# Attention of a hybrid diffusion step: heads in pairs on halves of the TensorE array, exponentials multiplied on VectorE

## What is computed

```python
def block_attention(q, k, v):
    ...
    scale = ATT_HD ** -0.5
    def one_block(qi):
        s = jnp.einsum('bqhgd,bkhd->bhgqk', qi, k, preferred_element_type=jnp.float32) * scale
        p = jax.nn.softmax(s, axis=-1).astype(v.dtype)
        return jnp.einsum('bhgqk,bkhd->bqhgd', p, v)
    ...
def odd_mixer(h, w_in, w_out, q_norm_w, k_norm_w, ctx_k=None, ctx_v=None):
    q, k, v = _split(h @ w_in, (ATT_Q, ATT_KV, ATT_KV))
    q = rmsnorm(q.reshape(b, t, ATT_HEADS, ATT_HD), q_norm_w)
    k = rmsnorm(k.reshape(b, t, ATT_KV_HEADS, ATT_HD), k_norm_w)
    ...
    if ctx_k is None:
        o = block_attention(q, k, v)
    else:
        q, k = axial_rope(q), axial_rope(k)
        o = block_attention(q, jnp.concatenate([ctx_k, k], axis=1), jnp.concatenate([ctx_v, v], axis=1))
    return o @ w_out, k, v
```

## Time and profile before

| | us |
|---|---|
| median of 3 runs | 3247.36 (3247.33 to 3247.4) |
| the profiled execution | 3248.14 |
| its span, first to last instruction | 3246.3 |
| TensorE busy | 3073.5 (95%) |
| VectorE busy | 1614.3 (50%) |
| ScalarE busy | 762.0 (23%) |
| GpSimd busy | 223.7 (7%) |

### The profile page before, as it was taken

How to read it: one execution, slowest core, us unless ns; L and a number is a source line. 1 busy time by engine, 2 the same in 40 slices (tenths; PEclk the granted TensorE clock), 3 DMA queues, 4 the chain that set the end, 5 groups by cost and what they waited for, 6 DMA issues and landing times.

```text
span 3246.3 us, 49355 instructions
## 1 busy us (share of the span) xinstructions
PE 3073.5 (95%) x20119; PEld 2896.3 (89%) x20119; DVE 1614.3 (50%) x2517; ACT 762.0 (23%) x939; POOL 223.7 (7%) x195
## 2 busy tenths in 40 slices
PE   7999998998989898999998999998989998999997
PEld 5999998998378888999998999998966668999997
DVE  6777565351355544777766752225343434222324
ACT  3212122222111122311222312113113442212122
POOL 2000000000033240000000000000003330000000
PEclk9999999996689989999999999999977998999999
DMA  7554332221000002355343332222100001222221
GB/s 242 156 156 142 120 118 76 75 67 47 10 1 1 0 8 78 116 156 151 124 139 107 116 96 73 78 72 71 65 31 1 1 1 52 65 78 78 66 71 52
DMA packets 306184, 256.04 MB, mean 79 GB/s; under 512 B 9100, under 2 KB 267272, under 8 KB 306056
## 3 DMA queue, kind: packets, MB, share of 16 engines
q1 hardware_dynamic: 306056, 254.26, 25.6%
HBM read 250.56 MB, written 3.67 MB: 78 GB/s over the span
## 4 chain that ended last, share of the span: by engine, by line
PE 90%; DVE 4%; issue 3%; ACT 2%; POOL 1%; DMA 0%; SPq 0%; DVEq 0%; POOLq 0%; ACTq 0%
PE ps L297 70%; PE ps L1593 2%; PE ps L1616 2%; PE ps L1286 2%; PE ps L709 2%; PE ps L1298 2%; PE ps L1296 1%; PE ps L1604 1%; PE ps L1063 1%; PE ps L736 1%; PE ps L1047 1%; PE ps L899 1%; POOL pr L1721 1%; PE ps L367 0%; PE ps L482 0%
## 5 line engine op out<-in xcount | busy, mean ns | idle before, releaser
L297 PE MATMUL ps<-h_hi,w_hi 128*128 128x320 f32 x3712 | 851.9, 311 | 22.7 <-DVE h_lo L533 16.4
L297 PE MATMUL ps<-h_lo,w_hi 128*128 128x320 f32 x3712 | 850.4, 310 | 0.0
L297 PE MATMUL ps<-h_hi,w_lo 128*128 128x320 f32 x3712 | 849.3, 310 | 0.0
L297 PEld LDWEIGHTS ps<-h_hi,w_hi 128*128 128x128 f32 x3712 | 624.4, 189 | 24.5 <-issue 24.4
L297 PEld LDWEIGHTS ps<-h_lo,w_hi 128*128 128x128 f32 x3712 | 625.3, 189 | 0.0
L297 PEld LDWEIGHTS ps<-h_hi,w_lo 128*128 128x128 f32 x3712 | 624.8, 189 | 0.0
L270 ACT CAST w_hi<-w_raw 128x2048 fp32r<-128x2048 f32 x164 | 311.6, 1900 | 542.9 <-PE ps L297 542.9
L277 DVE TENSOR_TENSOR w_lo<-w_raw,w_hi 128x2048 fp32r<-128x2048 f32 x164 | 375.5, 2290 | 92.1 <-ACT w_hi L270 91.8
L297 PE MATMUL ps<-hid_hi,w_hi 128*128 128x320 f32 x1408 | 321.8, 310 | 0.0
L297 PE MATMUL ps<-hid_lo,w_hi 128*128 128x320 f32 x1408 | 320.9, 309 | 0.0
L297 PE MATMUL ps<-hid_hi,w_lo 128*128 128x320 f32 x1408 | 320.6, 309 | 0.0
(11 more groups left out here) (241 smaller groups left out, 2663.0 us busy)
## 6 DMA issues: line engine op xcount, KB each, us to landing
w_raw<-in_ffn_w_in_dram SPq DMA_DIRECT2D x176, 512.0 KB, 5.0
mod_raw<-in_mod_w_dram SPq DMA_DIRECT2D x64, 1024.0 KB, 5.2
w_raw<-in_ffn_w_out_dram SPq DMA_DIRECT2D x64, 512.0 KB, 4.4
w_raw<-in_even_w_in_dram SPq DMA_DIRECT2D x28, 512.0 KB, 4.3
w_raw<-in_ffn_w_out_dram SPq DMA_DIRECT2D x32, 384.0 KB, 3.7
mod_first<-in_mod_w_dram SPq DMA_DIRECT2D x8, 1024.0 KB, 14.3
w_raw<-in_odd_w_in_dram SPq DMA_DIRECT2D x12, 512.0 KB, 4.3
w_raw<-in_even_w_out_dram SPq DMA_DIRECT2D x8, 512.0 KB, 4.1
```

Of the source, the lines that this page charges most:

```text
L297: mm = nc.tensor.matmul(ps[:, 4 * s + 2 * n + b, 0:HALF], w[s][:, k, cols], v[:, k, b * HALF:(b + 1) * HALF], start=(first and k == 0), st ...
```

## The change

Attention takes two heads at a time, the two of one query tile. For pair u (8 a block, 40 in all, written out without a loop):

- `scores` reads the queries straight from `proj` (no staging copy). The first head of the pair uses partitions 0 to 63 and banks 0 and 1, the second partitions 64 to 127 and banks 2 and 3; their matmuls alternate, in pieces of 256, 256 and 128 keys. They wait until both exponentials of pair u - 1 are done.
- The query norm's weight is multiplied by 1/8 once, ahead of the norms, so that the scores come scaled. VectorE's reduction writes the negated maximum itself; L1687 is gone.
- `exps` runs once for each head, into four buffers `pr`, which are now the scratch tiles `TMP`.
- `inverse` (VectorE) inverts a head's sum and multiplies the exponentials in place; `pool_attention` is gone.
- `turn` transposes both heads, ten tiles into banks 4, 5 and 7. ScalarE copies four tiles of the first head; VectorE the fifth of both, then four of the second.
- `values` alternates between the heads, which write partitions 0 to 63 and 64 to 127 of bank 6. The output is split every four pairs, 512 columns at a time.

```diff
-        q_st = over_u("q_st", [P, DT, P], 18432)
-        pt = [over_u(f"pt{s}", [P, 5 * P], 22528 + 2560 * s) for s in range(2)]
-        pr = [over_u(f"pr{s}", [P, 5 * P], 27648 + 2560 * s) for s in range(2)]
+        pt = [over_u(f"pt{s}", [P, 2, 5 * P], 22528 + 5120 * s) for s in range(2)]
+        pr = TMP
...
             dve.wait_ge(oc_in, 80)
+            nc.vector.tensor_scalar(qk_w[:, 0:1], qk_w[:, 0:1], ASCALE, None, ALU.mult).then_inc(qw_ready, 1)
             dve_tnorm_rec(dve, "odd_qk")
+            dve.wait_ge(qw_ready, 1)
...
+        PAIRS = AH // 2
+        UNITS = PAIRS * TT
...
+        def pair_pieces(kt):
+
+            if kt == 1:
+                return ((0, 0, P), (1, 0, P))
+            return ((0, 0, 256), (1, 0, 256), (0, 256, 512), (1, 256, 512), (0, 512, T), (1, 512, T))
...
+            def scores(u):
+                n, p, kt = pair_at(u)
+                if u == 0:
+                    pe.wait_ge(qr_step, 3 * DT)
+                else:
+                    pe.wait_ge(at_p, 2 * u)
+                for hh, c0, c1 in pair_pieces(kt):
+                    q = slice(64 * hh, 64 * hh + 64)
+                    k0 = P if n else 0
+                    mm = nc.tensor.matmul(psf[:, hh * 1024 + c0:hh * 1024 + c1], proj[q, p, n * P:(n + 1) * P],
+                                          keys[q, p // 2, k0 + c0:k0 + c1], start=True, stop=True)
                 mm.then_inc(at_s, 1)
...
+            def turn(u):
+                n, p, kt = pair_at(u)
+                pe.wait_ge(at_norm, 2 * u + 2)
+                if u:
+                    pe.wait_ge(at_ta, u)
+                    pe.wait_ge(at_td, u)
+                for hh in range(2):
+                    for i in range(kt):
+                        o = ((4 + hh) * 512 + i * P) if i < 4 else 7 * 512 + hh * P
+                        mm = nc.tensor.transpose(psf[:, o:o + P], pr[2 * (u % 2) + hh][:, i * P:(i + 1) * P], ident[:, :])
                 mm.then_inc(at_t, 1)
...
+                if p % 4 == 0 and u:
+                    pe.wait_ge(at_lo, u // 4)
+                o = 6 * 512 + (p % 4) * P
                 for i in range(kt):
+                    for hh in range(2):
+                        mm = nc.tensor.matmul(psf[64 * hh:64 * hh + HD, o:o + P],
+                                              vals[:, (1 + i if n else 0), (p // 2) * HD:(p // 2 + 1) * HD],
+                                              pt[u % 2][:, hh, i * P:(i + 1) * P], start=(i == 0), stop=(i == kt - 1))
                 mm.then_inc(at_o, 1)
...
+            scores(0)
+            for u in range(UNITS):
+                if u + 1 < UNITS:
+                    scores(u + 1)
+                turn(u)
+                if u:
+                    values(u - 1)
+            values(UNITS - 1)
...
+            def exps(u):
+                n, p, kt = pair_at(u)
+                for hh in range(2):
+                    h = 2 * p + hh
+                    act.wait_ge(at_neg, 2 * u + hh + 1)
+                    if u >= 2:
+                        act.wait_ge(at_t, u - 1)
+                    nc.scalar.activation(pr[2 * (u % 2) + hh][:, 0:kt * P], psf[:, hh * 1024:hh * 1024 + kt * P], ACT.Exp,
+                                         bias=a_neg[:, h:h + 1], accum_out=a_den[:, h:h + 1]).then_inc(at_p, 1)
...
+            def maxima(u):
+                n, p, kt = pair_at(u)
                 dve.wait_ge(at_s, u + 1)
+                for hh in range(2):
+                    h = 2 * p + hh
+                    nc.vector.tensor_reduce(a_neg[:, h:h + 1], psf[:, hh * 1024:hh * 1024 + kt * P], AX.X, ALU.max,
+                                            negate=True).then_inc(at_neg, 1)
+
+            def inverse(u, hh):
+                h = 2 * pair_at(u)[1] + hh
+                dve.wait_ge(at_p, 2 * u + hh + 1)
+                nc.vector.reciprocal(a_rec[:, h:h + 1], a_den[:, h:h + 1]).then_inc(at_rec, 1)
+                dve.wait_ge(at_rec, 2 * u + hh + 1)
+                v = pr[2 * (u % 2) + hh][:, 0:pair_at(u)[2] * P]
+                nc.vector.tensor_scalar(v, v, a_rec[:, h:h + 1], None, ALU.mult).then_inc(at_norm, 1)
...
+            for u in range(UNITS):
+                if u + 1 < UNITS:
+                    maxima(u + 1)
+                    inverse(u + 1, 0)
+                w = min(4, pair_at(u)[2]) * P
+                dve.wait_ge(at_t, u + 1)
+                if u >= 2:
+                    dve.wait_ge(at_o, u - 1)
+                if w > P:
+                    nc.vector.tensor_copy(pt[u % 2][:, :, 4 * P:5 * P], ps[:, 7, 0:2 * P].rearrange("p (h n) -> p h n", h=2))
+                nc.vector.tensor_copy(pt[u % 2][:, 1, 0:w], ps[:, 5, 0:w]).then_inc(at_td, 1)
+                if u + 1 < UNITS:
+                    inverse(u + 1, 1)
+                if u and u % 4 == 0:
+                    outputs(u // 4 - 1)
...
-            pool_attention(pool)
```

More of the change, by code:

```diff
@@ L1557, in dve_odd_prep @@
                 nc.vector.tensor_tensor(q, q, rt[j % 2][:, :], ALU.add).then_inc(qr_step, 1)
-        def blocks(eng, body):
-            body(0, None, 1, 5)
-            body(1, 1, 5, 5)
-            with eng.Fori(2, TT - 1) as n:
-                body(n, 5, 5, 5)
-            body(TT - 1, 5, 5, None)
-        def after(eng, s, v):
-            if not isinstance(v, int) or v > 0:
-                eng.wait_ge(s, v)
-        def unit(n, h, tk, tn):
-            return (n, h, tk) if h < AH else (n + 1, h - AH, tn)
@@ L1580, in pe_attention @@
-        def pe_attention(pe):
-            def scores(n, h, kt):
-                if kt is None:
-                    return
-                u = AH * n + h
-                if h == 0:
-                    pe.wait_ge(q_staged, n + 1)
-                after(pe, at_p, u - 1)
-                q = slice(64 * (h % 2), 64 * (h % 2) + 64)
-                o = 2 * (h % 2) * 512
-                k0, w = (0 if kt == 1 else P), kt * P
-                for c in range(0, w, 512):
-                    e = min(c + 512, w)
-                    mm = nc.tensor.matmul(psf[:, o + c:o + e], q_st[q, h // 2, :], keys[q, h // 4, k0 + c:k0 + e],
-                                          start=True, stop=True)
-                mm.then_inc(at_s, 1)
-            def turn(n, h, kt):
-                u = AH * n + h
-                pe.wait_ge(at_norm, u + 1)
-                after(pe, at_ta, u)
-                after(pe, at_td, u)
-                for i in range(kt):
-                    o = 4 * 512 + i * P
-                    mm = nc.tensor.transpose(psf[:, o:o + P], pr[h % 2][:, i * P:(i + 1) * P], ident[:, :])
+        PAIRS = AH // 2
@@ L1619, in values @@
                 mm.then_inc(at_o, 1)
-            def body(n, tp, tk, tn):
-                for h in range(AH):
-                    scores(*unit(n, h + 2, tk, tn))
-                    if h:
-                        values(n, h - 1, tk)
-                    elif tp:
-                        values(n - 1, AH - 1, tp)
-                    turn(n, h, tk)
             pe.wait_ge(ck_out, 1)
             pe.wait_ge(kr_step, 16)
-            for h in range(2):
-                scores(0, h, 1)
-            blocks(pe, body)
@@ L1716, in pool_attention @@
-        def pool_attention(pool):
-            def body(n, tp, tk, tn):
-                for h in range(AH):
-                    pool.wait_ge(at_rec, AH * n + h + 1)
-                    v = pr[h % 2][:, 0:tk * P]
-                    nc.gpsimd.tensor_tensor(v, v, a_rec[:, h:h + 1].to_broadcast([P, tk * P]), ALU.mult).then_inc(at_norm, 1)
-            blocks(pool, body)
+            scores(0)
[5 more added lines that the diff above has]
+                    values(u - 1)
@@ new lines, in pe_attention, with outputs @@
+            values(UNITS - 1)
+        def act_attention(act):
+            def exps(u):
[7 more added lines that the diff above has]
+                                         bias=a_neg[:, h:h + 1], accum_out=a_den[:, h:h + 1]).then_inc(at_p, 1)
+            def outputs(j):
+                n, t = j // 2, 4 * (j % 2)
+                act.wait_ge(at_o, 4 * j + 4)
+                nc.scalar.copy(h_hi[:, t:t + 4, n * P:(n + 1) * P],
+                               ps[:, 6, :].rearrange("p (t n) -> p t n", t=4)).then_inc(at_hi, 1)
+            exps(0)
+            for u in range(UNITS):
+                if u + 1 < UNITS:
+                    exps(u + 1)
+                w = min(4, pair_at(u)[2]) * P
+                act.wait_ge(at_t, u + 1)
+                if u >= 2:
+                    act.wait_ge(at_o, u - 1)
+                nc.scalar.copy(pt[u % 2][:, 0, 0:w], ps[:, 4, 0:w]).then_inc(at_ta, 1)
+                if u and u % 4 == 0:
+                    outputs(u // 4 - 1)
+            outputs(UNITS // 4 - 1)
@@ L1742, in pe_odd @@
             pe_attention(pe)
-            pe.wait_ge(at_lo, TT)
+            pe.wait_ge(at_lo, 2 * TT)
             pe_linear(pe, "odd_out", 4, None)
```

103 lines of the change are left out of this document (23 added, 80 removed).

## The result

The changed kernel takes **3143.03 us** (median of 4 runs, 3135.53 to 3144.01) against 3247.35 of the kernel before on the same chip: a ratio of **0.9676, 95% interval 0.966 to 0.9693**. The forecast was 3158 with a range from 3143 to 3195, so the direction was right, and the time lies at the very edge of the range's fast end: the gain is 104 us, and 89 were expected. The profiled run is the one of 3144.01 us.

A forecast was written before the change was run, and what follows sets the result against it. TensorE's phases were taken to bound the latent blocks, VectorE after the change. Context 22 + 32 pairs x 4.3 + clock 7 + end 3 = 169.6 us for a stage of 259.3, giving 3158 us; range 3143 to 3195.

The forecast's parts named there:

- The halves: Attention's matmuls on TensorE: both halves of the array overlap; a latent pair's scores 1.28 to 1.48 us, values 1.26.
- Score halves that take turns: Rival, 10%: row halves don't overlap in the scores; 5.2 us a latent pair, 3187 us in all (3180 to 3195).
- The rival of loads that show: Rival, 2%: each of a pair's 20 value records waits for its weight load; 5.7 us a pair, 3202 us.
- A latent round: One pair of heads in the latent blocks: 4.3 us expected against 6.42 for two heads before; ends 4.05 and 4.8.
- the loop through three engines: Latent pair: next scores wait for both exponentials; scores, first reduction, exponentials and way back take 4.03 us, 4.23 with overhang.
- two loops of nearly the same length that hand work to each other cost a little more than either: Latent pair: VectorE's 4.2 us and the way through the engines, 4.03 to 4.23, together taken as 4.3.
- The context block: First 8 pairs of attention, at the lower clock: 2.7 us a pair, 22 us in all against 28.
- The clock: Start of the latent blocks: clock still low for 2.5 pairs, 2.8 us extra each, 7 us; near full speed afterwards.
- The end: After the last latent pair: values, then the half-size split on ScalarE and VectorE one after another, 3 us.
- everything going well: Forecast's own fast end: 4.05 us a latent pair, 1.74 a context pair and an early clock rise, 3140 us.
- The slower case: Rival, 10%: clock stays low in the latent blocks; 7.7 us a pair, 3260 us (3232 to 3273).
- What would show it: Signs in latent rounds: multiplications 0.55 us, VectorE hardly idle, scores 1.3 to 1.5, values 1.2 to 1.3, rounds 4.2 to 4.4, GpSimd empty.

## Where the prediction was right and where not

*The halves.* Right: scores 1.35 (1.28 to 1.48 expected), values 1.31 (1.26), transposes 1.25 to the values (1.23). Score halves that take turns, the 10% rival, would need about 2.4; even head by head they took 1.89. The rival of loads that show is refuted in the round above: the pair's 20 loads of the whole height take 1.07 us beside 1.31 of matmuls. The Trainium skill ("TensorE: Matmul & The Clock Gate", Part 3, The mechanism) says that a weight load overlaps running matmuls only when its row group differs; these rows disagree with it too, since by it the values would have taken some 2.1 us more (an estimate, 20 loads of 0.106 us). The same section of the Trainium skill also has loads pulled ahead into a background weight buffer, which the rows would fit; no run here can show it.

*A latent round.* Right in kind: VectorE and the loop through three engines, 4.04 and 4.03 to 4.23 by the working, measured 4.03. "VectorE becomes the bound" came true by 0.06 us: the other loop is 3.97. A first step that failed is "two loops of nearly the same length that hand work to each other cost a little more than either": with the split they cost 4.18, which is VectorE's sum of 4.04 + 0.15, not 4.3. Term: 32 x 4.3 = 137.6, measured 133.8.

*The context block.* The step that failed here is the overlap: the term of 2.7 us a pair was too large. The timeline of one, at the lower clock:

```profile
2420.44 0.80 PE L1588 MATMUL ps<-keys,proj 64*128 64x128 f32 x4
...
2421.29 0.49 DVE L1665 TENSOR_REDUCE a_neg<-ps 128x1 f32<-128x128 f32 x2
2421.61 0.37 ACT L1637 ACTIVATE tmp_b<-ps,a_neg 128x128 f32<-128x128 f32 x1 [1.07 <-DVE a_neg L1665]
...
2422.47 0.80 PE L1588 MATMUL ps<-keys,proj 64*128 64x128 f32 x4
```

The round is 2.03: scores, first reduction (0.32 to the exponentials, not 0.5), exponentials. I had laid inverse, multiplication and copy end to end behind them; they lie beside the next round's scores. From the end of the rotation to the first latent scores at 2431.07 it is 16.6 us, 22 were expected.

*The clock.* Low through the context block, as expected, but it rose 2 us into the latent pairs (window 2433.20), not after 2.5 pairs. The first scores took 1.0 us more and one round 0.64 more: 1.6 us, not 7. The step that failed is to carry over the pace of the kernel before, where a head from 2459.00 on still took 6.02 us. Why the clock rose earlier is not shown; with the scores head by head it stayed low until 2440.40.

*The end.* 3 us were too few: behind the last full round come the last pair's multiplication, transposes, copies, values, cast and subtraction one after another, 7.0 us by what the other terms leave of the 159.0. From the last values (2570.46) to the output matmul it is the 3.0 that were expected; the steps ahead of them were put at nothing.

*Sum.* 16.6 + 133.8 + 1.6 + 7.0 = 159.0 for 22 + 137.6 + 7 + 3 = 169.6: context -5.4, rounds -3.8, clock -5.4, end +4.0. So of the 10.6 us the overlap in the context block and the clock's term are 5.4 each, the larger misses. The other 4 us lie outside the stage, 5.2 ahead of it less 1.0 behind, in the part that I treated as fixed: the three runs shown of before lay at 3247.33 to 3247.4, while the three larger samples have medians of 3243.38, 3244.24 and 3246.99 and single runs from 3234.55 to 3248.37. That they fell to the changed kernel's side is luck; its second profile was a run of 3148.59. Two hedges, "everything going well" left out of the range and one sample of the clock taken for all, put the range's fast end where the result came.

*The slower case.* The clock didn't stay low (1.00 from 2440 to 2572). *What would show it*: the multiplications of 0.55, rounds just under 4.2 to 4.4 and an empty GpSimd came as said.

## What to carry to other kernels

Find each loop that closes over a round, VectorE's own sum and the way through several engines back to a buffer, and take the longest as it is: here the working gave 4.03 to 4.04 us and the chip 4.03, and the allowances for overhang (0.2) and for the meeting of two loops (0.1) did not show. Where two loops are equal, relieving one is worth little until the other is shortened too: 3.4 and 1.4 us of the stage here, and 8.2 together. Take the time ahead of an edit from more than one profile before treating it as fixed, and compare versions by the stage they change.

## What the runs showed of the hardware

The two halves of the array need no strict alternation. Pieces alternating singly or by twos took 1.35 and 1.36 us, three and three 1.89; values in fives 2.02 for 1.31. In the last two, 0.8 and 0.6 us of the second head ran beside the first: a record for the free half started as soon as no more than three unstarted records for the other half stood ahead of it, in scores and values alike. So TensorE did not start its matmul records strictly in the order of its queue. Why three was not tried.

The granted clock in one unchanged stretch (the retention stage) differed between runs of one kernel, 54.6 us low in one and 34.1 + 10.2 in the other. Differences of this kind go with a place of the rotation that moved by up to 8.6 us over 13 profiles: by the trace's record of the clock it was at its lower level ahead of attention for 262.7 us in all where the rotation ended at 2411.05, and for 286.6 where it ended at 2419.69.
